# Merge and output stage of a hybrid layer: branch weights resident, units ordered branch by branch, output weights loaded during the attention and scaled by the gate

## The reference, cut to what matters

```python
def merge_branches(branches, merge_logits, w_br, w_out):
    gates = jax.nn.sigmoid(merge_logits)
    y = gates[..., :D_MODEL] * (branches[0] @ w_br[0])
    for i in range(1, N_BRANCH):
        y = y + gates[..., i * D_MODEL:(i + 1) * D_MODEL] * (branches[i] @ w_br[i])
    return y @ w_out
...
    x = x + gate * merge_branches([gm, na, rw, pl], zs['merge'], lp['w_br'], lp['w_out'])
...
    return rmsnorm(x, final_g)
```

## Time and profile before

| | us |
|---|---|
| median of 3 runs (lowest to highest) | 2600.18 (2587.19 to 2601.32) |
| the profiled execution's own time | 2595.6 |
| its span on the core | 2593.9 |
| PE busy in it | 2274.7 |
| DVE busy | 1598.2 |
| POOL busy | 188.2 |
| first merge matmul to the last output matmul | 2189.1 to 2585.7 |

### The profile page before, as it was taken

How to read it: one execution, slowest core, us unless ns; L and a number is a source line. 1 busy time by engine, 2 the same in 40 slices (tenths; PEclk the granted TensorE clock), 3 DMA queues, 4 the chain that set the end, 5 groups by cost and what they waited for, 6 DMA issues and landing times. The chain is left out here.

```text
span 2593.9 us, 65279 instructions
## 1 busy us (share of the span) xinstructions
PE 2274.7 (88%) x26450; PEld 1853.9 (71%) x26450; DVE 1598.2 (62%) x2618; ACT 1038.1 (40%) x1763; POOL 188.2 (7%) x260
## 2 busy tenths in 40 slices
PE   4999999999899999999577887777793997699998
PEld 2788878888688878888466766666573675577777
DVE  5756666667755465666376666665452675667865
ACT  5444234545421225444244554544323664222221
POOL 0000000000000000000311000100122820000000
PEclk8999999999999999999799999999795998899999
DMA  6343333332333323333301111110457104836742
GB/s 227 117 126 118 117 97 109 117 104 97 126 94 101 103 90 123 103 109 117 96 26 42 34 34 34 42 35 20 154 188 229 57 19 156 307 107 218 259 160 84
DMA packets 267469, 291.58 MB, mean 112 GB/s; under 512 B 33786, under 2 KB 193658, under 8 KB 264698
## 3 DMA queue, kind: packets, MB, share of 16 engines
q1 hardware_dynamic: 264954, 280.00, 33.6%
q10 hardware_dynamic: 2304, 8.39, 0.8%
HBM read 196.72 MB, written 91.61 MB: 111 GB/s over the span
## 5 line engine op out<-in xcount | busy, mean ns | idle before, releaser
L715 PE MATMUL proj_ps<-h_hi,w_hi 128*128 128x512 f32 x1656 | 649.8, 392 | 28.4 <-DVE h_lo L465 19.9
L716 PE MATMUL proj_ps<-h_lo,w_hi 128*128 128x512 f32 x1656 | 647.1, 391 | 0.0
L717 PE MATMUL proj_ps<-h_hi,w_lo 128*128 128x512 f32 x1656 | 646.4, 390 | 0.0
L318 ACT CAST w_hi<-w_raw 128x512 fp32r<-128x512 f32 x420 | 255.1, 621 | 695.2 <-PE proj_ps L717 353.0
L715 PEld LDWEIGHTS proj_ps<-h_hi,w_hi 128*128 128x128 f32 x1656 | 312.4, 189 | 98.7 <-issue 26.7
L717 PEld LDWEIGHTS proj_ps<-h_hi,w_lo 128*128 128x128 f32 x1656 | 312.3, 189 | 65.5
L716 PEld LDWEIGHTS proj_ps<-h_lo,w_hi 128*128 128x128 f32 x1656 | 312.6, 189 | 63.2
L482 DVE TENSOR_TENSOR w_lo<-w_raw,w_hi 128x512 fp32r<-128x512 f32 x420 | 283.1, 689 | 44.2 <-ACT w_hi L318 43.7
L498 DVE TENSOR_TENSOR z_slots<-proj_ps,x_rows 128x512 f32<-128x512 f32 x174 | 120.2, 691 | 170.1 <-PE proj_ps L717 168.0
L498 DVE TENSOR_TENSOR x_rows<-proj_ps,x_rows 128x512 f32<-128x512 f32 x116 | 80.1, 691 | 109.7 <-PE proj_ps L717 103.7
L2666 PE MATMUL late_ps<-mb_hi,mw_hi 128*128 128x512 f32 x256 | 103.8, 405 | 23.1 <-DVE mw_lo L2541 18.3
(11 more groups left out here) (347 smaller groups left out, 3987.3 us busy)
## 6 DMA issues: line engine op xcount, KB each, us to landing
w_raw<-in_w_in SPq DMA_DIRECT2D x240, 256.0 KB, 3.0
scratch_gatesT<-z_slots SPq DMA_DIRECT2D x128, 256.0 KB, 2.7
m_gate<-scratch_gatesT SPq DMA_DIRECT2D x64, 512.0 KB, 5.7
scratch_zT<-z_slots SPq DMA_DIRECT2D x108, 256.0 KB, 2.5
mw_rows<-in_w_br SPq DMA_DIRECT2D x32, 512.0 KB, 6.6
ada<-in_ada_w SPq DMA_DIRECT2D x4, 2048.0 KB, 15.4
mb_rows<-scratch_branchT SPq DMA_DIRECT2D x16, 512.0 KB, 7.3
x_res<-in_x SPq DMA_DIRECT2D x16, 512.0 KB, 4.5
```

The lines of the kernel that those rows point to most:

```text
L318: A.copy(wh[:, i, :, :], raw[:, q, :, :]).then_inc(w_hi, 1)
L715: T.matmul(out, wh[:, i, k, :], hi[:, o, k, :], start=(first and k == 0), stop=False, skip_group_check=not first)
L716: T.matmul(out, wh[:, i, k, :], lo[:, o, k, :], start=False, stop=False, skip_group_check=not first)
L717: last = T.matmul(out, wl[:, i, k, :], hi[:, o, k, :], start=False, stop=(k == 3), skip_group_check=not first)
```

## The change

It has these parts.

- The pooling work of the attention stage moves into a shared buffer `wo_rows`. As soon as it is over (`diff_set` 2) and the first part of the attention's rows has been stored, SP loads all eight pieces of the output weights into the same buffer, during the attention.
- The four branches' weights stay in SBUF: they are loaded, cast and subtracted once, 8 pieces in all. POOL subtracts those of branches 1 to 3, DVE those of branch 0.
- The output weights are multiplied by the gate row once, in place, before their cast: pieces 1, 3, 5, 7 by POOL, 0, 2, 4, 6 by DVE. `residual` then only adds. POOL forms all eight wo_lo.
- Units go branch by branch: for i, for p. Unit (i, p) uses PSUM slot p. The product is written over the gate piece itself, so the next gate piece for p is loaded only after the add. Branch inputs are two deep instead of four; those of branches 2 and 3 are subtracted by POOL in every block.
- A new queue of POOL instructions holds all its work in the order shown.
- ACT writes its squares to PSUM instead of a scratch buffer, and the next block's branch 0 units wait for them.

```diff
@@ -2061,7 +2061,7 @@
-        pp, s2, s4, s8 = (sb(n, [P, SEQ + 2 * EDGE]) for n in ("pool_in", "pool_2", "pool_4", "pool_8"))
+        pp, s2, s4, s8 = (s["wo_rows"][:, n * (SEQ + 2 * EDGE):(n + 1) * (SEQ + 2 * EDGE)] for n in range(4))
@@ -2128,6 +2128,10 @@
             for first, end in PARTS:
+                if first == PARTS[1][0]:
+                    sp.wait_ge(diff_set, 2)
+                    for m in range(KT):
+                        sp.dma_start(s["wo_rows"][:, m * D:(m + 1) * D], t["w_out"][0, m * P:(m + 1) * P, :]).then_inc(s["wo_in"], 16)
                 bvg.after(sp, end - 1, "g")
...
-        br, b_hi, b_lo = split("mb", [P, 8, BLK])
-        w, w_hi, w_lo = split("mw", [P, 2, 4, 2, 2 * P])
-        wo, wo_hi, wo_lo = split("wo", [P, KT, D])
+        wo, wo_lo = s["wo_rows"][:, 0:KT * D].rearrange("p (k n) -> p k n", k=KT), s["wo_lo"]
+        wo_hi = sb("wo_hi", [P, KT, D], F32R)
+        w, w_hi, w_lo = split("mw", [P, 4, 2, D])
         y, y_hi, y_lo = split("y", [P, KT, BLK])
-        gate, prod = sb("m_gate", [P, 4, 2, BLK]), sb("m_prod", [P, 2, 2, BLK])
-        xr = sb("x_res", [P, 2, D])
-        gb, fg, junk = sb("gate_rows", [P, D]), sb("final_g_rows", [P, D]), sb("out_junk", [P, D])
-        gcol = junk[:].rearrange("p (k m) -> p k m", k=KT)
+        br, b_hi, b_lo = split("mb", [P, 2, 2, BLK])
+        gate = sb("m_gate", [P, 4, 2, BLK])
+        xr, fg = sb("x_res", [P, 2, D]), sb("final_g_rows", [P, D])
+        gcol, gb = xr[:, 0, :].rearrange("p (k m) -> p k m", k=KT), xr[:, 1, :]
         ss, rt, rs = sb("out_ss", [P, 2]), sb("out_rt", [P, 2]), sb("out_rs", [P, 2])
...
+            sp.dma_start(w_part(w, 0, 0), w_brs[:, 0, :, 0:BLK]).then_inc(w_in[0], 16)
+            load_b(0, 0)
+            load_gate(0, 0, 0)
+            load_gate(0, 0, 1)
+            sp.dma_start(w_part(w, 0, 1), w_brs[:, 0, :, BLK:D]).then_inc(w_in[4], 16)
+            load_gate(0, 0, 2)
+            load_gate(0, 0, 3)
+            load_w(1)
+            load_b(0, 1)
+                for i in range(4):
+                    for p in range(NP):
+                        if p == 3 and (n, i) < (NB - 1, 2):
+                            sp.wait_ge(units, 16 * n + 4 * i + 4)
+                            load_b(*((n, i + 2) if i < 2 else (n + 1, i - 2)))
+                        if (n, i) < (NB - 1, 3):
+                            if i:
+                                sp.wait_ge(added, 12 * n + 4 * i - 3 + p)
+                            else:
+                                sp.wait_ge(gated, 16 * n + p + 1)
+                            load_gate(*((n, i + 1) if i < 3 else (n + 1, 0)), p)
+                        if n == 0 and i < 2 and p == 1:
+                            load_w(i + 2)
+                    if n == 0 and i == 1:
+                        sp.dma_start(fg[:], t["final_g"].rearrange("(a d) -> a d", a=1).to_broadcast([P, D])).then_inc(fg_in, 16)
+                    if i == 2:
+                        if n == 0:
+                            for by in range(2):
+                                sp.wait_ge(wo_s[by], KT // 2)
...
+        @block.gpsimd
+        def _(pool):
+            def split_b(n, i):
+                pool.wait_ge(b_h, 4 * n + i + 1)
+                G.tensor_tensor(b_lo[:, i % 2, :, :], br[:, i % 2, :, :], plain(b_hi[:, i % 2, :, :]), ALU.subtract).then_inc(b_lp, 1)
+            def split_w(i):
+                for h in range(2):
+                    pool.wait_ge(w_h, 2 * i + h + 1)
+                    G.tensor_tensor(w_part(w_lo, i, h), w_part(w, i, h), plain(w_part(w_hi, i, h)), ALU.subtract).then_inc(w_lp, 1)
+            def split_wo(first, end):
+                for k in range(first, end):
+                    pool.wait_ge(wo_h, k + 1)
+                    G.tensor_tensor(wo_lo[:, k, :], wo[:, k, :], plain(wo_hi[:, k, :]), ALU.subtract).then_inc(wo_l, 1)
+            pool.wait_ge(wo_in, 16 * KT)
+            pool.wait_ge(gb_set, 1)
+            for k in range(1, KT, 2):
+                G.tensor_tensor(wo[:, k, :], wo[:, k, :], gb, ALU.mult).then_inc(wo_s[1], 1)
+            split_w(1)
+            split_wo(0, 2)
+            split_w(2)
+            split_b(0, 2)
+            split_wo(2, 4)
+            split_w(3)
+            split_b(0, 3)
+            split_wo(4, KT)
+            for n in range(1, NB):
+                split_b(n, 2)
+                split_b(n, 3)
         @block.scalar
         def _(act):
...
             split_w(0, 0)
             split_b(0, 0)
+            split_w(0, 1)
+            for k in range(0, 4):
+                act.wait_ge(wo_s[k % 2], k // 2 + 1)
+                A.copy(wo_hi[:, k, :], wo[:, k, :]).then_inc(wo_h, 1)
+            split_w(1, 0)
+            split_w(1, 1)
             split_b(0, 1)
-            split_w(0, 1)
+            for k in range(4, KT):
+                act.wait_ge(wo_s[k % 2], k // 2 + 1)
...
-                dve.wait_ge(gate_in[i][m % 2], 16 * (m // 2) + 16)
-                to = prod[:, i % 2, :, :] if i else pair(y, m % NP)
-                V.tensor_tensor(to, gate[:, i, :, :], ps[:, i, :, :], ALU.mult).then_inc(gated, 1)
+            def multiply(n, i, p):
+                dve.wait_ge(gate_in[p][i % 2], 32 * n + 16 * (i // 2) + 16)
+                dve.wait_ge(units, 16 * n + 4 * i + p + 1)
+                to = gate[:, p, :, :] if i else pair(y, p)
+                V.tensor_tensor(to, gate[:, p, :, :], ps[:, p, :, :], ALU.mult).then_inc(gated, 1)
+            def add(n, i, p):
...
+                V.tensor_tensor(pair(y, p), pair(y, p), gate[:, p, :, :], ALU.add).then_inc(added, 1)
...
-                o = ps[:, g % 4, :, :]
-                vec.own(dve, g, V.tensor_tensor(o, o, gb[:].rearrange("p (b d) -> p b d", b=2), ALU.mult), "gated")
                 xv = xr[:, g % 2, :].rearrange("p (b d) -> p b d", b=2)
-                vec.own(dve, g, V.tensor_tensor(xv, xv, o, ALU.add), "res")
+                vec.own(dve, g, V.tensor_tensor(xv, xv, ps[:, g % 4, :, :], ALU.add), "res")
...
+            V.tensor_copy(gb.rearrange("p (b d) -> p b d", b=2), ps[:, 3, :, :]).then_inc(gb_set, 1)
+            dve.wait_ge(gb_set, 1)
+            dve.wait_ge(wo_in, 16 * KT)
+            for k in (0, 2):
+                V.tensor_tensor(wo[:, k, :], wo[:, k, :], gb, ALU.mult).then_inc(wo_s[0], 1)
+            split_w(0)
             split_b(0, 0)
-            split_b(0, 1)
-            split_w(0, 1)
-            split_b(0, 2)
-            split_b(0, 3)
-            dve.wait_ge(gb_set, 1)
+            split_w(1)
+            for k in (4, 6):
+                V.tensor_tensor(wo[:, k, :], wo[:, k, :], gb, ALU.mult).then_inc(wo_s[0], 1)
             for n in range(NB):
                 for p in range(NP):
+                    multiply(n, 0, p)
+                    if n and p == 1:
+                        normalise(4 * n - 1)
+                    if n == 0 and p == 1:
+                        split_b(0, 1)
+                for i in (1, 2):
+                    for p in range(NP):
+                        multiply(n, i, p)
+                        add(n, i, p)
+                for p in range(NP):
+                    multiply(n, 3, p)
+                    add(n, 3, p)
                     if p:
-                        split_y(m - 1)
-                    if n and p == 0:
-                        normalise(4 * n - 1)
-                    multiply(m, 2)
-                    add(m, 1)
-                    if m < LAST:
-                        split_w(m + 1, 0)
-                    multiply(m, 3)
-                    add(m, 2)
-                    add(m, 3)
-                    if m < LAST:
-                        split_w(m + 1, 1)
-                split_y(4 * n + 3)
-                if n == 0:
-                    for k in range(KT):
-                        split_wo(k)
+                        split_y(n, p - 1)
+                split_y(n, 3)
...
-                end_v.step(dve, V.tensor_tensor(o, o, gb[:, cols], ALU.mult))
-                end_v.step(dve, V.tensor_tensor(xr[:, 1, cols], xr[:, 1, cols], o, ALU.add))
+                end_v.step(dve, V.tensor_tensor(xr[:, 1, cols], xr[:, 1, cols], ps[:, 3, b, :], ALU.add))
...
+            def unit(n, i, p):
+                if n == 0 and i == 0:
+                    pe.wait_ge(w_l, p // 2 + 1)
+                    if p == 3:
+                        pe.wait_ge(gb_set, 1)
                 if p == 0:
-                    pe.wait_ge(b_l, 4 * n + i + 1)
+                    if n == 0 and i:
+                        pe.wait_ge(w_lp, 2 * i)
+                    if i < 2:
+                        pe.wait_ge(b_l, 2 * n + i + 1)
+                    else:
+                        pe.wait_ge(b_lp, 2 * n + i - 1)
+                if i:
+                    pe.wait_ge(gated, 16 * n + 4 * i - 3 + p)
+                elif n:
+                    sca.after(pe, 4 * n - 4 + p, "ss")
...
             for n in range(NB):
-                for p in range(NP):
-                    for i in range(4):
```

(28 more changed lines are left out.)

172 lines of the change are left out of this document (50 added, 122 removed).

## The result

The changed kernel takes 2581.9 us in the median of 15 runs, the kernel before 2596.3 beside it: a ratio of 0.994, 95% interval 0.993 to 0.995, so 14 us or 0.6% faster. Forecast were 2588, with 2580 to 2596 as the likeliest case's own range and 2562 to 2600 as the whole one. The profiled execution spans 2579.8 us, where that of before spans 2593.9.

What follows compares the result with a forecast made beforehand. PE was taken to bound the tiles, DVE nearly the merge, with holes in block 0. Terms -9.9, -0.7 and -2.2 sum to -12.8 us; on 2600.2 that is 2587.4, written as 2588, range 2562 to 2600.

Steps and rivals of the forecast that it cites:

- likeliest case: Whole kernel: the forecast itself, the engines taking turns in block 0, 2588 us, own range 2580 to 2596, chance 0.55.
- Weights once, branch by branch: Blocks 1 to 3: DVE keeps up without `mw_lo`; the 11.4 us excess goes, less 1.5: -9.9 us.
- The late `mb_lo`: Blocks 1 to 3: PE waits on `mb_lo`, 1.5 us in all; above 2 us would show the forecast wrong.
- that rival: Blocks 1 to 3: two-deep branch inputs late, 0 to 1.4 us six times, worst 8.4; up to 2597; chance 0.15.
- Gate multiply out of `residual`: Last stage: worth nothing in the tiles, one 0.70 us step on the path at the very end: -0.7 us.
- Output weights during the attention: Attention stage: SP's eight transfers have cover and touch no attention operand, costed at nothing.
- Block 0: Last stage's first block: POOL and DVE take turns on SBUF work; tile (0,1) at 2278.3, was 2280.5: -2.2 us.
- DVE's turn first: Block 0's start: with DVE before POOL, first matmul at 2198.7 instead of 2201, block 0 gains 4.5 us.
- the one to branch 1: Block 0: branch 0's matmuls last until 2214, four more pairs of turns end at 2215.7, where branch 1 starts.
- no exclusion: Block 0: POOL and DVE do not hinder each other, tile (0,1) at 2253, time 2562 us, chance 0.12.
- a fast POOL: Block 0: POOL takes 1.8 us per instruction, still in turns, time 2577 us, chance 0.12.
- the rounded output: Mostly block 0: POOL's subtraction costs double when writing the rounded format, time 2626 us, chance 0.06.

Runs made afterwards that it cites:

- e9: Kernel before, without DVE's 24 weight subtractions in blocks 1 to 3 (high part used twice, old order kept): 2583.0 us, ratio 0.994.
- e12: The changed kernel unaltered, profiled a second time: 2578.6 us, ratio 0.993.
- e7: Changed kernel without scaling the output weights; output tiles but the last multiplied in PSUM by the final norm's gains (gate left out): 2566.7 us, ratio 0.989.
- e2: Changed kernel with POOL waiting for DVE's first two weight subtractions, DVE scaling between products, ACT casting branch 1's weights earlier: 2576.5 us, ratio 0.992.
- e5: e4 with POOL's list sorted by when results are wanted, three output rows moved to DVE, ACT's casts reordered: 2570.8 us, ratio 0.990.
- e4: e2 plus branch 2's and 3's weight loads issued right behind branch 1's inputs: 2583.4 us, ratio 0.994 to the kernel before.
- e6: e5 with all eight output-weight scalings on DVE, none on POOL: 2565.2 us, ratio 0.987 to the kernel before.
- e11: e6 with all of GpSimd's work in the last stage given to DVE: 2574.7 us, ratio 0.991 to the kernel before.
- e8: Changed kernel plus eight extra 128x1024 DVE maximum operations in each of blocks 1 to 3: 2597.3 us, ratio 1.001 to the kernel before.
- e10: e6 with POOL making all eight output low parts, two before branch 3's inputs, and tile (0,0) taking y's low-part products last: 2570.7 us, ratio 0.989.

## Why the prediction was right, point by point

- *Weights once, branch by branch*, -9.9 us: right in its cause, with -7.5 and -9.3 in the two profiles. e9 shows the cause and the size of the excess. The late `mb_lo`, for which I had left 1.5 us, took 2.5 and 0.7 (over 2 us would show the term wrong, I had written; it did not reach the size of that rival, 1.4 us six times); some 1.6 us more than the matmuls alone stay in both profiles and in no listed wait (e12's matmuls there start 0.11 us late, 0.34 instead of 0.23 apart, at the start of branch 3 and within the tile behind it).
- *Gate multiply out of `residual`*: -0.7 us, and nothing in the tiles: right. DVE's tail is shorter by one 0.70 us step, and e7 shows the tiles to be no slower with a multiplication. The whole tail is 1.4 us shorter; the other 0.7 lies behind DVE's last instruction (3.9 us before, 3.2 after), and its cause stays open.
- *Output weights during the attention*: nothing, right (172.0 and 172.8 us without, 170.4 to 173.0 with). SP's eight issues took 6.7 us, where I had written some 4, but they had their cover.
- *Block 0*: the mechanism was right in all links but one, its size was not: -2.2 us (-4.5 with DVE's turn first), measured -9.3 and -9.4. DVE had the first turn. Counted from the stage's start, the links with DVE first stood at 18.2 (first product), 32.9, 51.2, 65.2 (branches 1 to 3), 81.2 and 95.5 (tiles (0,0) and (0,1)); they came at 17.1, 30.9, 48.1, 61.8, 76.2 and 90.6. The link that was wrong is the one to branch 1: PE did not wait there for turns, since branch 0's own matmuls, many of them at half the clock, took 13.9 us. The term that was mis-sized is the price of a pair of turns, 2.35 + 1.22 + 0.05 = 3.6 us: it measures 3.30, four scalings of POOL in 13.20. Some ten such pairs stand on the path to branch 2 and some six more on the way to tile (0,0): at 0.3 each 4.8 us, and 4.9 were to be explained. With POOL's 2.35, DVE's share of a pair is about 0.95, less than the 1.13 from one start to the next when it works alone; so the two overlap a little. The sums (L2596) that I expected up to 3.5 us long reached 2.2; `y_lo` reached 3.4.
- *Sum*: -12.8 forecast; -18.1 within the stage in the first profile, -20.1 in the second (its tail 6.7); -14.4 and -18.1 in the medians of the two comparisons. That the forecast is nearer to the first median than to its own terms is luck: the 4.0 us of the recurrence stage stood against the 5 us by which block 0 was mis-sized. Of the 6.1 us between 2588 and the measured 2581.9, 3.9 come from the time that I counted from: the median of three was 2600.2, that of fifteen is 2596.3. The second median, 2578.6, lies below the likeliest case's own range and within the whole one.
- *Rivals*: no exclusion and a fast POOL are refuted by e2 and by POOL's 2.4 us alone; the rounded output costs POOL nothing extra (`mb_lo` 2.34 to 2.42 alone, 2.35 assumed). The exclusion agrees with the Trainium skill, page SBUF — State Buffer, section Who interferes with whom: one engine waits for the other's instruction, both ways, and the products that read PSUM stayed at 1.21 us under POOL (1.22 at most in block 0). What I had not drawn from it is that the same rule says how to place the work.

## What to carry to other kernels

Before giving an engine a list of helper work, sort the list by when each result is wanted: in block 0 the same work in another order, three rows of it on VectorE, took 6.7 us less (e5 against e4), and an earlier start and an earlier transfer together had brought nothing before that (e4). Work with two SBUF inputs goes to VectorE first, where it has slack: a pair shared between the two engines costs 3.3 us, against 2 x 1.13 on VectorE. GpSimd's share still pays where VectorE has none left: it was worth 4 us in block 0 and 7 behind it (e6 against e11). And price a load on VectorE where its results fall due (the block's end here), not by the average of busy time.

## What the runs showed of the hardware

- Two engines in turns on two-input SBUF operations of 128x1024: POOL 2.35 us alone, DVE 1.22 alone with 1.13 from one start to the next, 3.30 for a pair. A DVE operation that reads PSUM keeps its 1.21 us.
- After the 12.5 us wait the matmuls start 0.43 us apart for 6 us and 0.23 apart from then on. The granted clock (the third number from the end) is 0.52 in the first stretch, near the 1.2 GHz level, and 1.00, the 2.4 GHz level, in the second:

```profile
2201.60:2208.00 6.40, 6.38 (x16) 5.00 (x17) 6.40 (x2) 0.95 (x2) 6.40 (x3) 0.52 0.01 3
2208.00:2214.00 6.00, 6.00 (x28) 4.96 (x27) 6.00 (x5) 4.00 (x4) 6.00 (x3) 1.00 0.03 8
```

The three waits of 4.1 us in e8 and the one of 3.6 in e10 were followed by such a stretch too, so these waits cost more than their own length.
- The same code ahead of the last stage (but for the eight transfers) ended between 2178.5 and 2190.4 us in fourteen profiles. An effect of a few microseconds in a late stage is read from the marks within that stage; the whole time shows it only through many runs.
